# One block for the whole program, with named waits where its stages meet, and a later square in the embedding stage

## What is computed

```python
for i in range(DEPTH):                       # first network, DEPTH = 2
    h = rms_norm(x, g_mix[i])
    ...                                      # the four branches, gated and summed: merged
    x = x + merged @ w_out[i]
    x = x + expert_choice_moe(rms_norm(x, g_moe[i]), w_router[i], ...)
    ple_gate = jax.nn.sigmoid(rms_norm(x, g_ple[i]) @ w_ple_gate[i])
    x = x + ple_gate * (p[i] @ w_ple[i])     # the embedding stage
x = rms_norm(x, g_final)
for layer in range(DEPTH):                   # second network
    x = x + (fox_mixer or hgrn2_mixer)(rmsnorm(x, g))
    x = x + conv_ffn(rmsnorm(x, ffn_norm_g[layer]), ...)
return rmsnorm(x, final_norm_g)
```

## Time and profile before

| | us |
|---|---|
| median of 3 executions | 3506.25 |
| lowest and highest | 3505.15, 3506.52 |
| profiled execution: span, which is also its own time | 3506.0 |
| TensorE busy | 3352.0 (96%) |
| VectorE busy | 1650.3 (47%) |
| ScalarE busy | 1152.8 (33%) |
| GpSimd busy | 96.0 (3%) |

### The profile page before, as it was taken

One profiled execution on the slowest core, in us unless ns is written; L12 is line 12 of the kernel. 1 busy time (PEld: TensorE's weight loads), 2 busy tenths in 40 slices (PEclk: granted clock), 3 DMA queues, 4 the chain that ended last, 5 costly groups with the idle time before them and its releaser, 6 DMA issues. The chain is left out here.

```text
span 3506.0 us, 41800 instructions
## 1 busy us (share of the span) xinstructions
PE 3352.0 (96%) x17328; PEld 2400.3 (68%) x17328; DVE 1650.3 (47%) x2514; ACT 1152.8 (33%) x1798; POOL 96.0 (3%) x79
## 2 busy tenths in 40 slices
PE   8999998999989989998999989999999999999998
PEld 6668875444447767876444447776788888778887
DVE  4564542212135574553121124435765675576665
ACT  5553322010125553232101014444533353443333
POOL 0000000000001000000000000000100010010000
PEclk9999998999989999998999999999999999999999
DMA  6122247999963112245999992321222222122222
GB/s 187 43 60 76 76 174 291 426 427 428 427 263 117 55 50 76 68 138 229 424 427 427 427 375 65 109 85 49 85 96 96 97 84 85 61 73 96 96 96 73
DMA packets 274939, 616.64 MB, mean 176 GB/s; under 512 B 10864, under 2 KB 210320, under 8 KB 225600
## 3 DMA queue, kind: packets, MB, share of 16 engines
q1 hardware_dynamic: 274224, 613.65, 46.2%
q10 hardware_dynamic: 528, 0.32, 0.0%
HBM read 609.71 MB, written 4.23 MB: 175 GB/s over the span
## 5 line engine op out<-in xcount | busy, mean ns | idle before, releaser
L456 PE MATMUL bank<-h_hi,w_hi 128*128 128x512 f32 x1784 | 710.1, 398 | 7.3 <-DVE w_lo L207 4.9
L458 PE MATMUL bank<-h_hi,w_lo 128*128 128x512 f32 x1784 | 697.1, 391 | 0.0
L457 PE MATMUL bank<-h_lo,w_hi 128*128 128x512 f32 x1784 | 696.9, 391 | 0.0
L207 DVE TENSOR_TENSOR w_lo<-w_raw,w_hi 128x2048 fp32r<-128x2048 f32 (+2 forms) x209 | 424.1, 2029 | 202.2 <-ACT w_hi L199 199.9
L2336 PE MATMUL bank<-expert_w,gathered 128*64 128x512 f32 x2016 | 446.8, 598 | 11.1 <-DMA expert_w<-in_w_exp_up 11.0
L199 ACT ACTIVATE w_hi<-w_raw 128x2048 fp32r<-128x2048 f32 (+2 forms) x209 | 355.5, 1701 | 236.3 <-PE bank L458 202.9
L456 PEld LDWEIGHTS bank<-h_hi,w_hi 128*128 128x128 f32 x1784 | 336.1, 188 | 96.2 <-issue 18.1
L458 PEld LDWEIGHTS bank<-h_hi,w_lo 128*128 128x128 f32 x1784 | 335.9, 188 | 72.0
L457 PEld LDWEIGHTS bank<-h_lo,w_hi 128*128 128x128 f32 x1784 | 336.3, 188 | 69.2 <-issue 1.9
L2336 PEld LDWEIGHTS bank<-expert_w,gathered 128*64 128x64 f32 x2016 | 143.9, 138 | 295.8 <-issue 289.9
L2336 PE MATMUL bank<-expert_w,hidden_t 128*64 128x512 f32 x1024 | 226.3, 595 | 0.0
(11 more groups left out here) (435 smaller groups left out, 4770.3 us busy)
## 6 DMA issues: line engine op xcount, KB each, us to landing
expert_w<-in_w_exp_up SPq DMA_DIRECT2D x64, 2048.0 KB, 22.0
expert_w<-in_w_exp_down SPq DMA_DIRECT2D x64, 2048.0 KB, 25.2
expert_w<-in_w_exp_gate SPq DMA_DIRECT2D x62, 2048.0 KB, 22.8
w_raw<-in_ffn_w_up SPq DMA_DIRECT2D x44, 1024.0 KB, 4.9
w_raw<-in_w_branch_gate SPq DMA_DIRECT2D x64, 512.0 KB, 3.8
w_raw<-in_w_in SPq DMA_DIRECT2D x22, 1024.0 KB, 5.1
w_raw<-in_ffn_w_down SPq DMA_DIRECT2D x22, 1024.0 KB, 4.8
w_raw<-in_hgrn_w_in SPq DMA_DIRECT2D x16, 1024.0 KB, 5.3
```

Of the source, the lines that this page charges most:

```text
L207: dve.tensor_tensor(self.w_lo[n % 2][:, 0:e], self.raw[n % self.RAW][:, 0:e], self.w_hi[n % 2][:, 0:e].bitcast(F32), ALU.subtract).then_in ...
L456: pe.matmul(out, st[0], mv[0], start=(j == 0), stop=False)
L457: pe.matmul(out, st[0], mv[1], start=False, stop=False)
L458: last = pe.matmul(out, st[1], mv[0], start=False, stop=(j == len(g.steps) - 1))
```

## The change

All stages share one `nc.Block()`, opened once (`v.block`), so no engine meets the others at a stage's end. Where the meeting had kept an order, a wait is named: TensorE waits for the bank's last user of an earlier stage (`v.bank_taken`), for the start stage's factors (`rstd_made`), for constants, and in the expert stage for the last row of `x`; SyncE waits for the mixer's last product before it loads expert tiles. Both feed-forward stages take banks 3 and 4 for their first two groups instead of 0 and 1.

In the embedding stage the tail of ScalarE works one group behind (`behind = 1`): sigmoid of row `kt`, then square and rounding of row `kt` - 1. The last square is in the next stage's start. `sums_row` and `spread_row` move later (2 and 4 to 5 and 7 for the second mixer; 1 and 5 to 3 and 7 for attention); `RawDoubleNorm.tail_pe` sums row `kt` - 2 behind group `kt`, and its last two rows are summed together at `sums_row`. The last square comes ahead of that row's rounding.

The diff without the lines that are only indented differently:

```diff
-        with nc.Block() as block:
+        block = v.block
...
                         if tail:
-                            tail.tail_act(act, first[n] + i)
+                        tail.tail_act(act, first[n] + i - tail.behind)
...
             def bank_free(pe, k):
                 b = self.before[k]
-                if b is not None:
-
+            if b is None:
+                for taken in v.bank_taken.get(id(self.bank[k]), ()):
+                    pe.wait_ge(*taken)
+                return
...
+        for k, bank in enumerate(self.bank):
+            v.bank_taken[id(bank)] = [act_took.ge(act_n[k]), dve_took.ge(dve_n[k])]
         sig.stage_end()
...
 class RawFeatureNorm(RawNorm):
-    in_tail, rests_in_tail, gathered_in_tail, sums_row, spread_row = 7, 6, 7, 2, 4
+    behind, in_tail, rests_in_tail, gathered_in_tail, sums_row, spread_row = 1, 7, 6, 7, 5, 7
...
 class StartNorm(Norm):
     def pe_before_tile(self, pe):
+        pe.wait_ge(*self.rstd_made)
         self.spread_to(pe, self.bank, self.v.rstd)
...
 class RawDoubleNorm(RawNorm, DoubleNorm):
-    in_tail, rests_in_tail, sums_row, spread_row = 7, 6, 1, 5
+    behind, in_tail, rests_in_tail, sums_row, spread_row = 1, 7, 6, 3, 7
+
+    def tail_pe(self, pe, k):
+        kt = self.kt_of.get(k)
+        if kt is not None and kt >= 2:
+            self.part(pe, kt - 2)
...
     def act_start(self, act):
+        self.square(act, KT - 1)
         self.raw_high(act, KT - 1)
         self.root_table(act)
-        DoubleNorm.act_start(self, act)
+        self.roots(act)
...
     def sums(self, pe):
+        self.part(pe, KT - 2)
         self.part(pe, KT - 1).then_inc(*self.summed.inc())
...
+    norm.rstd_made, v.constants_here = norm.rstd.own(), loaded.own()
     sig.stage_end()
...
+        tiles[1].pre_act = tiles[1].pre_dve = lambda eng: eng.wait_ge(*v.constants_here)
+        tiles[1].needs = v.constants_here
...
+    loads.mixer_products = sig("group_summed").own()
     return loads, after
...
             @block.sync
             def _(sp):
+            sp.wait_ge(*loads.mixer_products)
                 for g in (0, *range(loads.EARLY + 1, RING + 1)):
...
+            pe.wait_ge(*norm.added(KT - 1))
                 norm.logits(pe, KT - 1).then_inc(*logits.inc())
...
-        dense = Dense(v, None, tiles, banks=v.ps[0:7], ring=v.ring)
+        dense = Dense(v, None, tiles, banks=v.ps[0:7], ring=v.ring, first_banks=v.ps[3:5])
...
+        with nc.Block() as v.block:
         with first:
```

More of the change, by code:

```diff
@@ new lines, in run, with _ @@
+        block = v.block
+        @block.gpsimd
+        def _(p):
+            if lead:
+                lead.pool_start(p)
+            if pool:
+                pool(p)
+            if tail:
+                tail.tail_pool(p)
+        @block.sync
+        def _(sp):
+            for n in range(count):
+                ring.load(sp, n0 + n, tiles[n].srcs)
+                if after_load and n >= ring.RAW:
+                    after_load(sp, n)
+            for i, srcs in enumerate(following):
+                ring.load(sp, n0 + count + i, srcs)
@@ new lines, in _ @@
+        @block.tensor
+        def _(pe):
+            if lead:
+                lead.pe_start(pe)
+            for n, t in enumerate(tiles):
+                if lead and n == lead.tile:
+                    lead.pe_before_tile(pe)
+                pe.wait_ge(*ring.lo_ready(n0 + n))
+                if t.needs:
+                    pe.wait_ge(*t.needs)
+                if lead and n in ((lead.tile, lead.tile + 1) if raw else (lead.tile,)):
+                    if raw and n == lead.tile:
+                        raw_tile_by_rows(pe)
+                    else:
+                        first_tile_by_rows(pe, n)
+                    for k in range(first[n], first[n + 1]):
@@ new lines, in start_stage, with _ @@
+    block = v.block
+    @block.sync
+    def _(sp):
+        for i in range(4):
+            sp.dma_start(v.x[:, 2 * i:2 * i + 2, :], v.io["x_t"].rearrange("(k p) t -> p k t", p=P)[:, 2 * i:2 * i + 2, :]).then_inc(*x_loaded[i].dma())
+        first, second = mixer_first(v)
+        v.ring.load(sp, 0, first)
+        for dst, src in v.const_loads[2:]:
+            sp.dma_start(dst, src).then_inc(*loaded.dma())
+        v.ring.load(sp, 1, second)
+        sp.wait_ge(*loaded.ge(16 * len(v.const_loads[2:])))
@@ new lines, in _ @@
+    @block.tensor
+    def _(pe):
+        pe.wait_ge(*tables.ge(32))
+        for i in range(2):
+            pe.matmul(v.ps[3 + i][:], table[:], onehot[:, i * S:(i + 1) * S], start=True, stop=True).then_inc(*made.inc())
+        pe.wait_ge(*early.ge(48))
+        norm.sums(pe)
+    @block.scalar
+    def _(act):
+        for dst, src in ((table[:], v.io["rel_rep"]), (onehot[:], v.io["c_onehot"])):
+            act.dma_start(dst, src).then_inc(*tables.dma())
+        for dst, src in v.const_loads[0:2] + [(v.gains[:], v.io["gains"])]:
+            act.dma_start(dst, src).then_inc(*early.dma())
+        for kt in range(KT):
+            norm.square(act, kt)
+        act.wait_ge(*early.ge(48))
+        norm.root_table(act)
+        norm.root(act)
+        v.ring.high(act, 0)
@@ new lines, in moe, with _ @@
+        block = v.block
+        @block.sync
+        def _(sp):
+            sp.wait_ge(*loads.mixer_products)
+            for g in (0, *range(loads.EARLY + 1, RING + 1)):
+                if g == 6:
+                    sp.wait_ge(*norm.summed.ge(1))
+                loads.issue(sp, g)
+            for g in range(RING + 1, NP * NT):
+                sp.wait_ge(*at(used, 0, g - RING + 1))
+                loads.issue(sp, g)
+            sp.wait_ge(*at(used, 0, NP * NT - 4))
+            small.load_p(sp)
+            for n, srcs in enumerate(small.first):
+                v.ring.load(sp, v.ring.tiles + n, srcs)
@@ L2429, in moe, with _ @@
+        @block.tensor
+        def _(pe):
+            tensor_router(pe)
+            for q in range(2):
+                tensor_gather(pe, 0, q)
+            for i in range(NP):
+                tensor_pair(pe, i)
         for s, n in per.items():
```

931 lines of the change are left out of this document (426 added, 505 removed).

## The result

The changed kernel takes 3480.89 us (median of 4 executions, 3479.27 to 3484.42), the kernel before 3505.70 on the same chip (3502.88 to 3506.52): ratio 0.9926, interval 0.9913 to 0.9939. The forecast was 3480.7 in a range of 3473 to 3492.

What follows compares the result with a forecast made beforehand. TensorE, busy 96% of the span, bounds the kernel, so only its idle time and slow stretches can be won. Terms of 0.3 + 0.6 + 3.8 + 6.9 + 5.6 + 3.2 + 3.3 + 1.6 = 25.3 us off 3506.0 gave 3480.7, range 3473 to 3492.

Steps and rivals of the forecast that it cites:

- The first rival: Stage boundaries: norm factors hanging on the last row set every start in the meeting's place; 8 us less gain, 3488.7, chance 0.16.
- The slower rival: Long stretches without a wait: the chip grants less clock to a TensorE that hardly stops; 3521 at 80 us, chance 0.03.
- The rival of the slow drip: Scatters from experts to embedding: two products per addition stay at low clock and give nothing; 3484.5, chance 0.10.
- Start to mixer: First mixer's start: gain 0.3 us, ScalarE's wait on the weights' path, though TensorE waited 2.4; bounds 0 and 2.4.
- Mixer to experts: Two boundaries: TensorE waits for the last addition to `x` instead of the meeting; 0.6 us in all, bounds 0 and 0.6.
- Experts to embedding: Two boundaries: scatter starts on the expert output's low part, with slow drips priced in; 1.9 us each, 3.8 in all.
- First embedding stage to mixer: Unnormed products start at once, ending 5.73 us idle and 1.6 of slow clock; 6.9 us taken, bounds 4.5 and 7.3.
- a spare of 1.2 us: First embedding stage's end: slack in the last-row chain, so GpSimd's addition beside VectorE's multiply and add was costed at nothing.
- Inside the second embedding stage and its end: Wait for row 0's square and slow clock go, 5.6 us; idle and slow products into attention go, 3.2 us.
- Feed-forward boundaries: Into and out of feed-forward stages, three times: idle 1.2 us each, no slow clock; 3.3 us in all, lower bound 0.9.
- Last stage: Final sums: sixteen of 24 small products start 1.8 us sooner, the last eight wait for the last square; gain 1.6 us.
- The term with the wrong form: Slow clock behind waits at scatters, embedding stages and their ends: an idle stretch costs its length, then part of what follows.

Runs made afterwards that it cites:

- the block alone: Shared block and named waits kept, embedding stage's order of squares and sums as before, against the kernel before: 3497.04 us, ratio 0.9971.
- the sums early: Changed kernel with the sums into the mixer back behind row 2 and the factors' rows behind row 4: 3485.19 us, ratio 0.9936 to the kernel before.
- the two pairs of traces: Kernel before and changed kernel, each profiled, then profiled again unchanged; the repeats took 3502.23 us (one execution) and 3477.12 us.
- the order: Kernel before with its old blocks and only the embedding stage's new order of squares and sums: 3500.34 us, ratio 0.9984.

## Why the prediction was right

The direction and the mechanism hold point by point. The meetings were idle time that TensorE need not have had: no `PEq` wait is left, L390 starts 0.23 us behind the last product at clock 1.00, L820 waits for nothing, the scatter waits 1.73 us for its first operand. The first rival (the factors take the meeting's place) would have shown a wait at the sums or at L413 of the raw tiles, and there is none. It did come true where the change was made by halves: with the block alone, and with the sums early. The slower rival is refuted: mean clock 0.983 before, 0.986 after. The rival of the slow drip stays half open: the first scatter's drip was slow in both traces, and this boundary gave 2.4 and 1.4 us in its row, but 4.4 and 0.3 to the stage's end.

The sizes, forecast and measured in the two pairs of traces:

- Start to mixer, 0.3: 0.3 on the path that I named. The wait at L538 fell from 2.4 to 0.6 us, but the wait for the first high part behind it grew from 1.7 to 3.2, so L413 starts at 19.93, where L411 started at 20.22: ScalarE's and VectorE's weights moved by 0.3 and no more. What comes of it hangs on the clock behind: 14 products ran 0.43 us apart in the changed kernel's trace and 8 in the other.
- Mixer to experts, 0.6: 0.6.
- Experts to embedding, 3.8: 5.6 and 4.6 in the table's rows, 6.1 and 1.9 with the rest of the stage. The order of events is as forecast. The drip was slow as priced at the first boundary and fast at the second, which gave 3.2, near the upper bound of 3.4; but the stretch at half clock behind the small sums, which I had not looked for, takes 1.6 of it. I had priced what each boundary gives up to the scatter's end, and not what follows it.
- First embedding stage to mixer, 6.9: 7.4 and 7.5. VectorE's path to the third tile's low weights did not hold it back: TensorE waits 0.61 us for it there, where it had waited 0.55 for ScalarE. The step that failed is the last row: I had it 2 us behind TensorE's last product and it was 3.3 us, as VectorE's addition took 1.67 us beside GpSimd's. I had seen the overlap and costed it at nothing, because of a spare of 1.2 us, and 0.1 was left. The rows show more than a slowdown: VectorE's addition ended 0.55 us behind the end of GpSimd's (1088.39 and 1087.84), as if it had done little until then, and does so at another row, where GpSimd's took longer (1083.07 and 1082.52). The Trainium skill, "SBUF — State Buffer", "SBUF: two separate sides", has it so for a VectorE instruction with two SBUF inputs: of the two, the one that starts first holds the port and the other blocks. By it the price could have been estimated, as what is left of GpSimd's addition when VectorE's begins, 1.1 us; 0.98 was measured.
- Inside the second embedding stage and its end, 8.8: 9.3 and 8.1.
- Feed-forward boundaries, 3.3: 4.4 and 4.4. Each is 1.05 of the last row's addition and 0.4 of the block's end. I had counted the row's idle time alone (1.20). But a product overlaps the one before it by 0.39 - 0.23 = 0.16 us, which a stop takes away, and the first pair behind a stop took 0.54 us for 0.46: 0.24 more for each of these stops. Behind small products the same counting gives only 0.12 (1.59 lost for 1.47 idle, with the last row waited for at the end of the second embedding stage).
- Last stage, 1.6: 1.6 and 1.5.

**What was luck.** The sum of 25.3 is 3.5 too small for the first pair of traces (28.8): in the table's rows the scatters have 1.8 more than forecast, the feed-forward boundaries 1.1 and the two embedding stages 0.5 each. It looks right for the second pair (3500.4 - 3475.7 = 24.7), but there the rows add up to 26.8, and the rest went in stretches that the forecast does not speak of. And I took the span of the profiled execution for its time. In the runs that list both, the time is 1.7 to 2.2 us more than the span (1.7 to 1.9 with the old blocks), so the base was some 1.8 us too low. The two errors pull against each other.

**The term with the wrong form** is the clock. I had read 1.5 + 1.6 + 2.1 + 0.9 + 1.4 us from the one trace and put them into the sum as if a wait had a fixed price. The repeats show a price of 0 to 3.0 us for one and the same wait. The drip is the plainest case. The Trainium skill, "TensorE: Matmul & The Clock Gate", "HAM oscillation", tells of short bursts that run slow again and again, in a kernel that waits 3 to 5 us between them; here the wait is 1.7 us, and the burst was slow in four traces and fast in three. So the price belongs into the range, as a chance. Why it falls sometimes is not settled: no run here controlled the moment at which a wait begins.

## What to carry to other kernels

Where the parts of a change share a path, price them together and alone: the block was worth 9 us, the order 6, both 25 to 31, and the distances show 8 us that come only from both, because each took away only the wait that hid the other's. Follow such a distance far enough: half of one gain was given back some 70 to 90 matmuls behind the boundary. Compare short stretches between the same two instructions in both traces; where the clock is the same they repeat to 0.05 us, and medians of whole runs scatter by 4. And look at what stands in front of the wait that is left: an engine's order of work (here 1.9 us of ScalarE ahead of what TensorE waited for) was there before the change, and worth as much as a boundary.

## What was not expected of the hardware

- The same wait of 2.65 us was followed by 3.0, 1.6 or 0 us of loss to the lower clock in three executions. Shorter idle time isn't always less loss: 4.0 us were followed by 6.4 us of work at 0.51, while 5.73 us had been followed by 3.5 us at 0.52.
- A VectorE addition of 128x512 from two SBUF operands took 1.67 us beside GpSimd's addition and 0.69 alone; five of the eight in the first embedding stage did so and took 1.66 or 1.67 us, the other three 0.69. Each of the five ended 0.55 us behind GpSimd's addition, as here:

```profile
1081.05 1.47 POOL L663 TENSOR_TENSOR ple_squares<-ple_squares 128x512 f32<-128x512 f32 x1 [4.09 <-ACT ple_squares L510]
1081.41 1.66 DVE L2561 TENSOR_TENSOR x<-x,ple_gate 128x512 f32<-128x512 f32 x1
```

  Before, none of the eight fell beside one, as GpSimd's six additions stood elsewhere.
- A block's end costs about 0.4 us beyond the wait for the last addition, at the three feed-forward boundaries, where it was taken apart.
- A stretch of 3.4 us at half clock can follow small products although TensorE did not stop at them: behind the norm's 24 sums (2.7 us, one column each) it came in both embedding stages of all twelve traces of kernels with the block, the order or both, and in one of four of the kernel before. In some of these kernels TensorE also waited for GpSimd within the sums; in the changed kernel it did not. What sets the stretch is open.
